# Strassen steps in four of eight weight steps of every couple, weights split into a ring of seven places

## The reference

```python
u = rms_norm(h, norm_mlp_g[i])
h = h + jnp.square(jax.nn.relu(u @ mlp_w1[i])) @ mlp_w2[i]      # mlp_w1 2048 x 8192, mlp_w2 8192 x 2048
gate = jax.nn.sigmoid(rms_norm(h, ple_norm_g[i]) @ ple_w_gate[i])
h = h + gate * (p[i] @ ple_w_proj[i])
```

## Time and profile before

| | |
|---|---|
| median of 3 runs | 1185.73 us (1185.48 to 1185.89) |
| profiled execution, its own time | 1186.18 us |
| its span, first to last instruction | 1184.4 us |
| PE busy | 1176.9 us (99%) |
| DVE busy | 827.9 us (70%) |
| ACT busy | 635.5 us (54%) |
| mean granted PE clock | 0.999 |

### The profile page before, as it was taken

How to read it: one execution, slowest core, us unless ns; L and a number is a source line. 1 busy time by engine, 2 the same in 40 slices (tenths; PEclk the granted TensorE clock), 3 DMA queues, 4 the chain that set the end, 5 groups by cost and what they waited for, 6 DMA issues and landing times.

```text
span 1184.4 us, 14269 instructions
## 1 busy us (share of the span) xinstructions
PE 1176.9 (99%) x5417; PEld 978.0 (83%) x5417; DVE 827.9 (70%) x1141; ACT 635.5 (54%) x882; POOL 22.5 (2%) x31
## 2 busy tenths in 40 slices
PE   9999999999999999999999999999999999999998
PEld 7888888888888888888888888888888888888886
DVE  5568876888776667755788755879655888676554
ACT  6745455666656565543565543456533566455443
POOL 1000100000000000000000000000000000000000
PEclk9999999999999999999999999999999999999999
DMA  9867663333348665865477865476854577886661
GB/s 341 322 178 242 215 235 139 108 108 134 109 162 281 210 215 199 279 233 194 146 244 250 273 214 191 176 247 232 285 195 178 192 243 241 273 258 208 217 207 44
DMA packets 110980, 249.26 MB, mean 210 GB/s; under 512 B 9664, under 2 KB 55744, under 8 KB 110912
## 3 DMA queue, kind: packets, MB, share of 16 engines
q1 hardware_dynamic: 110768, 248.34, 61.9%
q10 hardware_dynamic: 144, 0.01, 0.0%
HBM read 233.63 MB, written 14.68 MB: 210 GB/s over the span
## 4 chain that ended last, share of the span: by engine, by line
PE 99%; DMA 0%; DVE 0%; SPq 0%; ACT 0%; issue 0%
PE acc L1786 59%; PE acc L1812 11%; PE tr L1812 7%; PE sc L1786 7%; PE sc L1812 6%; PE sc L2013 1%; PE sc L1978 1%; PE tr L1930 1%; PE tr L1919 0%; PE sc L1919 0%; PE tr L2066 0%; PE tr L2065 0%; DMA w_raw<-in_nsa_w_in_units_dram 0%; PE acc L1902 0%; PE tr L2042 0%; PE tr L2043 0%
## 5 line engine op out<-in xcount | busy, mean ns | idle before, releaser
L1176 DVE TENSOR_TENSOR w_split<-w_raw,w_split 128x1024 fp32r<-128x1024 f32 x296 | 358.7, 1220 | 211.6 <-ACT w_split L733 210.9
L733 ACT ACTIVATE w_split<-w_raw 128x1024 fp32r<-128x1024 f32 x296 | 309.7, 1057 | 255.3 <-PE acc L1786 194.3
L1786 PE MATMUL acc<-w_split,b_split 128*128 128x512 f32 x1536 | 355.3, 390 | 0.0
L1786 PEld LDWEIGHTS acc<-w_split,b_split 128*128 128x128 f32 x1536 | 287.3, 188 | 59.1
L1786 PE MATMUL acc<-w_split,a_hi 128*128 128x512 f32 x1020 | 318.1, 393 | 1.6 <-DVE w_split L1172 1.6
L1786 PEld LDWEIGHTS acc<-w_split,a_hi 128*128 128x128 f32 x1020 | 188.6, 188 | 40.9 <-issue 2.4
L1786 PE MATMUL acc<-w_split,a_lo 128*128 128x512 f32 x510 | 198.9, 390 | 0.0
L744 ACT ACTIVATE w_split<-w_raw 128x1024 fp32r<-128x1024 f32 x95 | 97.6, 1052 | 44.4 <-PE acc L1786 20.9
L1190 DVE TENSOR_TENSOR w_split<-w_raw,w_split 128x1024 fp32r<-128x1024 f32 x78 | 93.3, 1217 | 31.3 <-ACT w_split L744 31.3
L1786 PEld LDWEIGHTS acc<-w_split,a_lo 128*128 128x128 f32 x510 | 95.7, 188 | 20.3
L1812 PE MATMUL acc<-w_split,a_hi 128*128 128x512 f32 x298 | 91.7, 389 | 0.0
(11 more groups left out here) (253 smaller groups left out, 1091.3 us busy)
## 6 DMA issues: line engine op xcount, KB each, us to landing
w_raw<-in_mlp_w_units_dram SPq DMA_DIRECT2D x256, 512.0 KB, 4.4
w_raw<-in_nsa_w_in_units_dram SPq DMA_DIRECT2D x76, 512.0 KB, 4.6
w_raw<-in_nsa_w_out_units_dram SPq DMA_DIRECT2D x32, 512.0 KB, 4.2
w_raw<-in_ple_w_gate_units_dram SPq DMA_DIRECT2D x32, 512.0 KB, 4.3
turn_dram<-s SPq DMA_DIRECT2D x52, 128.0 KB, 3.4
turn_dram<-junk SPq DMA_DIRECT2D x44, 128.0 KB, 3.5
v_slc<-turn_dram SPq DMA_DIRECT2D x22, 256.0 KB, 3.8
v_win<-turn_dram SPq DMA_DIRECT2D x22, 256.0 KB, 4.6
```

The source lines that it names most:

```text
L733: nc.scalar.activation(w_hi[:, u % SPLIT], w_raw[:, u % RAW], ACT.Copy).then_inc(hi_done, 1)
L1176: nc.vector.tensor_tensor(w_lo[:, u % SPLIT], w_raw[:, u % RAW], f32(w_hi[:, u % SPLIT]), ALU.subtract).then_inc(lo_done, 1)
L1786: last = nc.tensor.matmul(banks_of(c)[t][:], xs[:, kt, toks], ws[:, u % SPLIT, m * NW:(m + 1) * NW], start=(kt == 0 and n == 0), stop=(kt ...
```

## The change

- **Four Strassen steps in every couple**, k = 3, 4, 5, 6: 28 in all where there were 17.
- **Items.** What is split is now numbered in one row (`ITEM`, `T_ITEM`): a unit is one item, and a Strassen step adds two more, its weight sums. `lo_done` and `unit_used` count items. In a step the four items are used for 2, 1, 2 and 2 products.
- **Seven places.** `t_split` no longer belongs to the sums: its room gives three places more to the ring. From the first Strassen step on (`WIDER`) an item may be rounded once PE has finished the one seven before it.
- **Sums.** They go to two buffers `w_sums`, which lie in the upper half of `b_split`, in three instructions (1024, 512 and 512 columns) where there were four of 512 in `w_raw`. Those of a step stand one step earlier in DVE's queue: the first behind unit 5, the others behind the halved unit of the step before. `w_raw` is freed without waiting for them.
- **Squares in place.** `hidden_out` squares in `mixed`, and the turned blocks use `v_slc` and `v_win`; `stage`, `junk` and `s1` are left out.
- **Later in the queues.** `pair_sums` goes from behind unit 2 to behind unit 5, `hidden_out` to units 6 and 7, `turn_hidden` to 7 and 8 (down part: 7 and 9), `turned_hidden` in the down part to 13 and 15 on DVE, and the transfers that belong to them move on SP. `add_to_h` moves by three to five units. The load of `p_raw` goes to the last down part. The rounding of `r_split` stands one unit later.

```diff
-QUADS = (2, 4, 6)
+QUADS = (3, 4, 5, 6)
 N_QUADS = len(QUADS)
 def quads(c):
-    return QUADS if (c - C_MLP) % 8 == 0 else QUADS[1:]
+    return QUADS
...
+ITEM, T_ITEM = {}, {}
+def _number_items():
+    n = 0
+    for u in range(UNITS + 1):
+        ITEM[u] = n
+        n += 1
+        if u - 1 in QUAD_UNITS:
+            T_ITEM[u - 1] = (n, n + 1)
+            n += 2
+    return n
+N_ITEMS = _number_items()
+END.update({c: ITEM[u] for c, u in END.items() if c >= C_MLP})
+WIDER = ITEM[QUAD_UNITS[0]]
+PLACES = (SPLIT, SPLIT + 1, SPLIT + 2, *((WIDER + n) % SPLIT for n in range(SPLIT)))
+def place(item):
+    return item % SPLIT if item < WIDER else PLACES[(item - WIDER) % len(PLACES)]
+def place_free(item):
+    if WIDER <= item < WIDER + len(PLACES) - SPLIT:
+        return 0
+    return item + 1 - (SPLIT if item < WIDER else len(PLACES))
...
+        with nc.sbuf_tensor("w_sums", [P, 2, 2, 2, UW], F32) as w_sums:
...
-                    sp.wait_ge(lo_done, raw_free(u - RAW))
+                    sp.wait_ge(lo_done, ITEM[u - RAW] + 1)
...
+            def place_hi(item, src, at=0):
+                if place_free(item):
+                    act.wait_ge(unit_used, place_free(item))
+                hi, _ = weights(item)
+                nc.scalar.activation(hi[:, at:UW], src, ACT.Copy).then_inc(hi_done, 1)
             def split_hi_pair(c):
                 for s in range(2 * UPC):
                     u = FIRST[c] + s
                     act.wait_ge(raw_full[u % RAW], 16 * (u // RAW + 1))
...
                 n, mixes = PAIR_NO[c], pair_banks(c)[1]
-                act.wait_ge(quad_used, QUADS_TO[c])
+                act.wait_ge(unit_used, T_ITEM[FIRST[c] + 2 * quads(c)[-1]][1] + 1)
+                if n:
+                    act.wait_ge(blocks_turned, TT * (T_HID + (c - C_MLP) // 8 * 4 + (c - C_MLP) % 8))
...
-                    nc.scalar.activation(stage[:, t], mixed[:, 2 * half + t], ACT.Square).then_inc(squared, 1)
+                    nc.scalar.activation(src, src, ACT.Square).then_inc(squared, 1)
...
-                        if s in (3, 5):
-                            hidden_out(c - 2, s // 2 - 1)
+                        if s in (6, 7):
+                            hidden_out(c - 2, s - 6)
...
+            def place_lo(item, src, at=0):
+                dve.wait_ge(hi_done, item + 1)
+                hi, lo = weights(item)
+                nc.vector.tensor_tensor(lo[:, at:UW], src, f32(hi[:, at:UW]), ALU.subtract).then_inc(lo_done, 1)
+            def weight_sums(u):
+                at, n, q = QUAD_UNITS.index(u), u % RAW, (u - FIRST[C_MLP]) // (8 * UPC)
+                raw = w_raw[:, n:n + 2].rearrange("p u (m j) -> p (u m) j", m=2)
+                b21, b22 = raw[:, 1], raw[:, 3]
+                one_three = weight_sum(at, 0).rearrange("p (m j) -> p m j", m=2)
+                two, four = (weight_sum(at, 1)[:, m * NW:(m + 1) * NW] for m in range(2))
+                dve.wait_ge(raw_full[n], 16 * (u // RAW + 1))
+                dve.wait_ge(raw_full[n + 1], 16 * (u // RAW + 1))
+                if q:
+                    dve.wait_ge(unit_used, END[C_MLP + 8 * q - 1])
+                if at >= 2:
+                    dve.wait_ge(lo_done, T_ITEM[QUAD_UNITS[at - 2]][1] + 1)
+                nc.vector.tensor_tensor(one_three, raw[:, 0:4:3], raw[:, 2:3].broadcast_to([P, 2, NW]), ALU.add)\
+                  .then_inc(sums, 1)
+                dve.wait_ge(sums, 3 * at + 1)
+                nc.vector.tensor_tensor(two, one_three[:, 0], b22, ALU.add).then_inc(sums, 1)
+                dve.wait_ge(sums, 3 * at + 2)
+                nc.vector.tensor_tensor(four, two, b21, ALU.add).then_inc(sums, 1)
             def split_lo_pair(c):
                 for s in range(2 * UPC):
                     u = FIRST[c] + s
...
+                    if u - 1 in QUAD_UNITS:
+                        place_lo(ITEM[u], w_raw[:, u % RAW, NW:UW], NW)
+                        at = QUAD_UNITS.index(u - 1)
+                        if u - 1 != FIRST[c] + 2 * quads(c)[-1]:
+                            weight_sums(QUAD_UNITS[at + 1])
+                        for m, item in enumerate(T_ITEM[u - 1]):
+                            place_lo(item, weight_sum(at, m))
+                    else:
+                        place_lo(ITEM[u], w_raw[:, u % RAW])
...
+                    if not p and s == 2 * quads(c)[0] - 1:
+                        add_to_h(c - 1, 3)
+                    if s == 2 * quads(c)[0] - 1:
+                        weight_sums(FIRST[c] + s + 1)
...
-                        if s == 2:
+                        if s == 5:
                             pair_sums(c - 2)
-                        if s in (4, 6):
-                            turn_hidden(n + s // 2 - 2)
+                        if s in (7, 8):
+                            turn_hidden(n + s - 7)
...
-                own, sums_of = (w_hi, w_lo), (t_hi, t_lo)
                 start, stop = k == quads(c)[0], k == quads(c)[-1]
                 c11, c21, c12, _ = banks
                 one, five, six, seven = mixes
-                pe.wait_ge(direct, at + 1)
-                product(one, tile_rows(2 * k, 0), split(own, u % SPLIT, 0), start, stop)
-                product(c11, tile_rows(2 * k + 1, 0), split(own, u % SPLIT, 1), False, False)
+                pe.wait_ge(lo_done, own[0] + 1)
+                product(one, tile_rows(2 * k, 0), split(own[0], 0), start, stop)
+                product(c11, tile_rows(2 * k + 1, 0), split(own[0], 1), False, False).then_inc(unit_used, 1)
+                pe.wait_ge(lo_done, own[1] + 1)
                 pe.wait_ge(r_done, 1)
-                product(c12, combined(3), split(own, (u + 1) % SPLIT, 1), False, False).then_inc(unit_used, 2)
-                pe.wait_ge(lo_done, u + 2)
-                product(c21, tile_rows(2 * k + 1, 1), split(sums_of, 1, 1), False, False)
-                product(five, combined(0), split(sums_of, 1, 0), start, stop)
-                product(six, combined(1), split(sums_of, 0, 1), start, stop)
-                product(seven, combined(2), split(sums_of, 0, 0), start, stop).then_inc(quad_used, 1)
+                product(c12, combined(3), split(own[1], 1), False, False).then_inc(unit_used, 1)
+                pe.wait_ge(lo_done, rest[0] + 1)
+                product(five, combined(0), split(rest[0], 0), start, stop)
+                product(seven, combined(2), split(rest[0], 1), start, stop).then_inc(unit_used, 1)
+                pe.wait_ge(lo_done, rest[1] + 1)
+                product(six, combined(1), split(rest[1], 0), start, stop)
+                product(c21, tile_rows(2 * k + 1, 1), split(rest[1], 1), False, False).then_inc(unit_used, 1)
```

More of the change, by code:

```diff
@@ L127 @@
 QUAD_UNITS = [FIRST[c] + 2 * k for c in PAIR_NO for k in quads(c)]
-QUADS_TO = {c: sum(len(quads(b)) for b in PAIR_NO if b <= c) for c in PAIR_NO}
-def raw_free(u):
-    return u + 2 if u in QUAD_UNITS else u + 1
+UNITS = FIRST[C_PLE] + 4 * (1 + UPC)
+ITEM, T_ITEM = {}, {}
[18 more added lines that the diff above has]
+    return item + 1 - (SPLIT if item < WIDER else len(PLACES))
 T_KS, T_KW, T_H1 = range(3)
@@ L224, in trunk_layer @@
             pass
[L225 to L229 removed]
+        with nc.sbuf_tensor("t_split", [P, 2, len(PLACES) - SPLIT, UW], F32R) as t_split:
+            with nc.sbuf_tensor("r_split", [P, 2, 4, N_QUADS, P], F32R) as r_split, \
+                    nc.sbuf_tensor("mixed", [P, 4, NW], F32) as mixed:
+                pass
+            with nc.sbuf_tensor("p_raw", [P, 2, SEQ], F32) as p_raw, \
+                    nc.sbuf_tensor("pt_hi", [P, 2, SEQ], F32R) as pt_hi, \
+                    nc.sbuf_tensor("pt_lo", [P, 2, SEQ], F32R) as pt_lo:
+                pass
         t_hi, t_lo = t_split[:, 0], t_split[:, 1]
@@ L391, in pair_banks, with weights, weight_sum @@
             return tr + mlp_acc[1], mlp_acc[0] + sc
+        def weights(item):
+            n = place(item)
+            return (x[:, n % SPLIT] for x in ((w_hi, w_lo) if n < SPLIT else (t_hi, t_lo)))
+        def weight_sum(at, m):
+            return w_sums[:, at % 2, 1, m]
         def quad_tiles(x, n):
@@ L767, in hidden_out @@
                 n = PAIR_NO[c]
-                t_set = T_HID + (c - C_MLP) // 8 * 4 + (c - C_MLP) % 8 + half
-                act.wait_ge(blocks_turned, TT * t_set)
                 for t in range(TT):
@@ L1043, in _ @@
                     turned_gain(T_H1, a_hi, 0, GAIN_MLP)
-                if k == 0:
-                    act.wait_ge(p_full, 16)
-                    nc.scalar.activation(pt_hi[:], p_raw[:], ACT.Copy).then_inc(p_hi, 1)
                 if k == 3:
@@ L1089, in down_pair @@
                 for s in split_hi(FIRST[c + 2], 2 * UPC):
-                    if s in (3, 5):
-                        hidden_out(c, s // 2 - 1)
-                    if s in (10, 13):
-                        turned_hidden(s // 3 - 1, q)
+                    if s in (6, 7):
+                        hidden_out(c, s - 6)
+                    if s in (12, 14):
```

(15 more changed lines are left out.)

180 lines of the change are left out of this document (71 added, 109 removed).

## The result

The changed kernel takes **1189.21 us** (median of 7 runs, 1188.75 to 1189.64), the kernel before 1185.73 (7 runs, 1185.48 to 1186.52). The ratio is 1.003, with a 95% interval of 1.0018 to 1.0041: 3.5 us slower, with eleven products less to compute. The forecast was 1190.2, in a range of 1187.0 to 1193.5.

The account below looks back on a forecast made before the run. PE, busy 1176.9 of 1184.4 us, bounds the kernel, DVE next. Against the profiled 1186.18: +6.15 (B) + 0.33 (C) - 2.0 (A) = +4.5, 1190.7; less 0.45 to the median, 1190.2 us; range 1187.0 to 1193.5.

Parts of the forecast that it names:

- The products: PE in all couples: eleven products fewer at 0.6805 us save 7.49 us; an unheld couple takes 40.83 us.
- DVE's prices: DVE per Strassen step: splits 4.02 us, sums 2.58; wide add of 1024 columns 1.22, bounds 0.69 and 1.45.
- the rival that DVE pays full lengths: DVE: no instruction starts before the one ahead ends; +8.5 us, 1198.7; chance 0.03.
- B's queue: Couple B: 33.14 us of DVE work up to k = 5's first sums item; PE waits 3.4 us; three B, +6.15.
- The 0.15 for ACT: Couple B: DVE's short wait for ACT, which has `hidden_out` ahead of the halved unit of k = 3; estimated 0.15 us.
- C and A: Couple C waits 1.7 us at k = 5 only, 42.52 us, +0.33; couple A never waits, 2.3 us reserve, -2.0 in all.
- the term of -0.67 for each A: Couple A: one product fewer and no wait, 0.67 us shorter in each of three, together -2.0.
- The edits at nothing: Down parts and moved transfers, `turned_hidden`, `r_split`, `p_raw`: hidden behind PE's work, 0 us.
- the ring covers all: Rival: seven items in hand prevent every wait; 1178.2 us, or 1182.1 in a weaker form; chance 0.09 together.
- only one of B's waits stays: Rival: DVE's queue to k = 4 is 1.6 us shorter, B waits 1.8, C not; 1183.6 us; chance 0.11.
- the turned blocks come late: Rival: SP's queue uses up the 5 us reserve before B's unit 15; each B 3 us longer, 1199; chance 0.04.
- PE's clock: Rival: after each of seven waits a Strassen step runs at half rate; +33 us, 1223; chance 0.03.

Follow-up runs that it names:

- the load put into B on purpose: Changed kernel plus two chained DVE adds of 512 columns, result unused, in couple B behind unit 8: 1193.96 us, ratio 1.0072 to the kernel before.
- the 1.46 put there: Changed kernel plus two chained DVE adds of 512 columns (1.46 us), result unused, in couple A behind unit 8: 1189.30 us.
- the k = 3, 4, 5 version: Changed kernel with Strassen steps only at k = 3, 4, 5 in couples B and C, four kept in A: 1184.90 us, ratio 0.9994 to the kernel before.

## Why the prediction was right, step by step

**The products.** 0.6805 us a product, eleven fewer. A is 40.80 for a forecast of 40.83: right. The profile puts the product at 0.680; over seven couples that is 0.2 us.

**DVE's prices.** The wide add with its repeated operand takes 1.22 or 1.23, as taken from the line through 384 and 1536 columns, and neither of the bounds. A set of sums takes 2.60 (613.37 to 615.97) for 2.58, `pair_sums` 2.39 for 2.39, six units 6.80 for 6.84. By the same rows the rival that DVE pays full lengths falls: 617.16 to 617.76 is 0.60 for an add recorded with 0.68, and 614.63 to 615.36 is 0.73 where a semaphore lies between. The Trainium skill's statement weighed in the prediction (VectorE: DVE Perf Modes, "The DRAIN you can't avoid"), that the semaphore adds nothing, is again not what this trace shows.

**B's queue.** The chain was forecast as 33.14 us from 1.95 ahead of B's start. It starts 1.95 ahead (606.57 against 608.52) and ends at 639.61: 33.04. PE goes on 31.14 behind B's start for a forecast of 31.33. The two waits were forecast as 1.6 and 1.8; listed are 1.26 and 1.55, lost are 1.55 and 1.83. B is 44.19 for 44.26, and the load put into B on purpose came out at 1.47 of 1.46: shown, not only argued. The 0.15 for ACT was there, at the place that was named, as 0.13. That B came out within 0.07 is in part luck, for small misses cancel: the chain is 0.10 shorter than the sum, and PE goes on 0.05 behind it and not 0.14, but each row behind a wait takes 0.12 more, which the sum didn't have.

**C and A.** C waits once, at k = 5, and takes 42.52 for 42.52. A doesn't wait; its first item of sums of k = 5 is ready 25.7 us behind A's start for a forecast of 25.6, so that the reserve is 2.2 for 2.3. It covered the 1.46 put there, and a ring of five used it up.

**What was off.** Summed against the profiled execution the forecast was +4.5, and +3.0 came. Half of that is the program's start, 0.75 earlier in the profiled run of the changed kernel, which the change doesn't touch; the correction of 0.45 between profiled run and median took in a part of it, so that the median is only 1.0 off. 0.3 is the short hold in the third A of the kernel before, which the sum took for one like the first: the term of -0.67 for each A was measured as -0.71, -0.73 and -1.01. The last part is 0.05 us a B, 0.04 to 0.06 an A, and rounding. The edits at nothing were nothing: no wait at the down parts, and none of PE for ACT or a transfer. The bounds of the range don't follow exactly from their terms: 1190.2 + 3.0 is 1193.2, and 1.0 off the queue in three B and in C gives 1186.2. The measured time is far from both.

**The rivals.** That the ring covers all falls with the seven waits. That only one of B's waits stays falls too; the k = 3, 4, 5 version shows such a B, at the price of 1.55 for its one wait. That the turned blocks come late has no wait that would bear it out. PE's clock stayed at 1.00 in the 2 us behind each of the seven waits.

## What to carry to other kernels

When an engine at 100% is relieved, count the next engine's queue item by item up to each thing that the first one waits for, from an anchor that the change doesn't move; the busy share of a stage (here 40.8 to 44.1 us) says that there will be waits, the queue says where and how long. A Strassen step in place of a plain one saves PE 0.68 us (4.76 for 5.44) and costs DVE 4.3 (6.6 for 2.3). A saving of this kind pays only as often as the next engine has slack, and in this kernel late in the stage rather than early: four such steps in A, which still leave DVE 6 us idle, and three in B, which leave it 2, k = 4, 5 and 6 and not 3, 4 and 5.
